# Sharing the tile products of a chunked gated-delta scan between its two directions

## What is computed

```python
def gated_delta_chunked(q, k, v, g, beta, s0):
    # chunks of C tokens; gc = cumsum(g) in a chunk
    decay = exp(where(incl, gc[:, None] - gc[None, :], -inf))
    kb = kc * bc[..., None]
    a_low = where(strict, einsum('cd,sd->cs', kb, kc) * decay, 0)      # key products
    tmat = a_low + eye(C)
    w = solve(tmat, kb * exp(gc)[..., None]); u = solve(tmat, vc * bc[..., None])
    qk = einsum('cd,sd->cs', qc, kc) * decay                           # query-key products
    kd = kc * exp(g_last - gc)[..., None]
    def step(s, ...):
        v_new = u_i - w_i @ s
        o = qg_i @ s + qk_i @ v_new
        s = s * exp(gl_i) + kd_i.T @ v_new
o_forward  = gated_delta_chunked(q, k, v, g[0], beta[0], s)
o_backward = reversed(gated_delta_chunked(reversed q, k, v, g[1], beta[1], s))
```

## Time and profile before

| | |
|---|---|
| runs | 1705.11, 1707.46 and 1711.45 us; median 1707.46 |
| profiled execution | 1704.45 us, span of its instructions 1702.3 us |
| mean granted TensorE clock | 0.983 of full speed |
| busy in the span | TensorE 1618.2 us, VectorE 734.4, ScalarE 466.6, GpSimd 569.8 |
| HBM traffic | 307.31 MB read, 14.71 MB written |
| scan of layer 0 | from about 357 us of the span to about 520 |
| scan of layer 1 | from about 1250 us to 1364 |

### The profile page before, as it was taken

How to read it: one execution, slowest core, us unless ns; L and a number is a source line. 1 busy time by engine, 2 the same in 40 slices (tenths; PEclk the granted TensorE clock), 3 DMA queues, 4 the chain that set the end, 5 groups by cost and what they waited for, 6 DMA issues and landing times. The chain is left out here.

```text
span 1702.3 us, 36038 instructions
## 1 busy us (share of the span) xinstructions
PE 1618.2 (95%) x14725; PEld 1108.7 (65%) x14725; DVE 734.4 (43%) x1515; ACT 466.6 (27%) x1042; POOL 569.8 (33%) x698
## 2 busy tenths in 40 slices
PE   6999999889999999999999999999979999999998
PEld 4577875557887865555556447786668986555544
DVE  4257543345545451121111546744456675224233
ACT  4212433253333131111111231253353322111111
POOL 2656304226566213111110155611538881000000
PEclk9999999999999989999999999999989999999999
DMA  9330100069884249999999302010220035899995
GB/s 337 91 115 26 50 15 28 13 191 289 253 269 176 75 176 338 372 359 360 357 342 344 110 25 75 25 50 17 63 85 24 15 124 209 336 413 407 411 413 227
DMA packets 160358, 323.73 MB, mean 190 GB/s; under 512 B 30153, under 2 KB 118127, under 8 KB 144879
## 3 DMA queue, kind: packets, MB, share of 16 engines
q1 hardware_dynamic: 127584, 287.20, 45.8%
q0 software_dynamic: 7008, 21.74, 4.6%
q10 hardware_dynamic: 25646, 13.12, 2.8%
HBM read 307.31 MB, written 14.71 MB: 189 GB/s over the span
## 5 line engine op out<-in xcount | busy, mean ns | idle before, releaser
L1531 PE MATMUL psum<-ring,arena 128*64 128x256 f32 x1536 | 172.8, 381 | 6.8 <-DVE arena L3131 3.4
L1531 PEld LDWEIGHTS psum<-ring,arena 128*64 128x64 f32 x1536 | 108.6, 137 | 68.3 <-issue 13.4
L3642 POOL DMA_INDIRECT big<-h_rows_lat,idx x16 | 15.7, 981 | 346.1 <-PE psum L1664 174.0
L802 PE MATMUL psum<-hT,ring 128*128 128x256 f32 (+2 forms) x496 | 130.2, 421 | 0.0
L3152 DVE TENSOR_TENSOR arena<-arena,psum 128x384 f32<-128x384 f32 (+1 forms) x32 | 15.6, 487 | 257.6 <-PE psum L1540 158.5
L802 PEld LDWEIGHTS psum<-hT,ring 128*128 128x128 f32 (+1 forms) x496 | 92.7, 188 | 36.9 <-issue 26.6
L3190 DVE SCALAR_TENSOR_TENSOR xT<-psum,modraw,xT 128x512 f32<-128x512 f32 (+1 forms) x136 | 79.7, 621 | 48.6 <-PE psum L1618 33.8
L975 PE MATMUL psum<-hT,ring 128*128 128x256 f32 (+1 forms) x192 | 80.0, 525 | 0.0
L2444 ACT COPY arena<-psum 128x512 f32<-128x512 f32 (+2 forms) x49 | 23.7, 483 | 202.5 <-PE psum L1553 143.4
L1614 PE MATMUL psum<-arena 128*128 128x512 f32 x144 | 65.8, 602 | 4.4 <-DVE arena L3177 2.7
L2754 DVE TENSOR_REDUCE small<-psum 128x1 f32<-128x768 f32 (+1 forms) x40 | 33.9, 849 | 82.3 <-PE psum L996 82.2
(11 more groups left out here) (476 smaller groups left out, 3771.7 us busy)
## 6 DMA issues: line engine op xcount, KB each, us to landing
ring<-in_moe_w_gate SPq DMA_DIRECT2D x64, 1024.0 KB, 9.6
ring<-in_ada_w SPq DMA_DIRECT2D x48, 1024.0 KB, 7.1
ring<-in_moe_w_up SPq DMA_DIRECT2D x32, 1024.0 KB, 10.3
hT<-in_moe_w_down SPq DMA_DIRECT2D x24, 1024.0 KB, 12.7
ring<-in_w_in SPq DMA_DIRECT2D x20, 1024.0 KB, 5.5
big<-in_moe_w_up SPq DMA_DIRECT2D x16, 1024.0 KB, 10.9
sz<-in_moe_w_down SPq DMA_DIRECT2D x16, 1024.0 KB, 12.5
big<-in_moe_w_down SPq DMA_DIRECT2D x16, 1024.0 KB
```

The source lines that it names most:

```text
L802: m = pe.matmul(b[0:c1 - c0, 0:n], lhsT=w[:, k, c0:c1], rhs=hT[:, k, t0:t0 + n], start=k == 0, stop=k == KD - 1)
L1531: m = pe.matmul(b[e * CAP_L:(e + 1) * CAP_L, 0:2 * P], lhsT=xs[:, k, e, 0:CAP_L], rhs=w[e][:, 2 * (k - ks[0]) + q, :], start=k == 0, stop= ...
```

## The change

Three kinds of products are made once for two chunks that use the same tiles. `SHARED` lists them with the first of the two chunks: in layer 0 kr and qk of chunk 0 (used again in chunk 1) and kk of chunk 3 (used again in chunk 4); in layer 1 kk of chunk 3 alone. In the first chunk TensorE makes the product as before; ScalarE copies it from PSUM into a part of mixT that isn't written yet (`kept`), at the beginning of the slot in which TensorE makes it, and the bank is free with that copy. VectorE reads the copy in SBUF, in both chunks. In the second chunk TensorE makes nothing. Waits that asked for a bank to be read ask the semaphore "comb" instead, which VectorE increments after each such piece, and the counts of its earlier users are shifted. Two new waits order the reuse of mixT: ScalarE waits for the reads of qk before it puts kk of chunk 3 there, and VectorE's outputs of chunks 2 and 3 wait for its own reads of kr and kk.

```diff
+SHARED = ((("kr", 0), ("qk", 0), ("kk", 3)), (("kk", 3),))
...
+        def shared_steps(l):
+            order = [x for j in range(NT) for slot in range(len(BETWEEN)) for x in between(j, slot)]
+            return [(what, i, d) for what, i, d in order for w, j in SHARED[l] if what == w and i in (j, j + 1)]
+
+        def kept(l, what, j, d):
+            i = tile_of(d, j)
+            row, col = 2, {"kr": (2, 5), "qk": (3, 4)}.get(what, (0, 1))[i] if i < CT else i
+            if i >= CT and what != "kk":
+                row, col = GH * (what == "qk"), i - CT - 1
+            return mixT[:, row:row + GH, col * P:(col + 1) * P]
+
+        def product_kept(l, what, j):
+            return (what, j) in SHARED[l]
+
+        def product_shared(l, what, j):
+            return (what, j - 1) in SHARED[l]
+
+        def factor_made(eng, l, what, j, d):
+            if product_kept(l, what, j) or product_shared(l, what, j):
+                base = sum(1 + IN_PAIRS + len(shared_steps(x)) for x in range(l)) + 1 + IN_PAIRS
+                eng.wait_ge(sems[l]["comb"], base + shared_steps(l).index((what, j, d)) + 1)
+            else:
+                evacuated(eng, (what, l, j, d))
```

In TensorE's pieces:

```diff
+                    if product_shared(l, what, j):
+                        return
...
-                        evacuated(pe, ("qk", l, j, d))
+                        factor_made(pe, l, "qk", j, d)
...
-                        evacuated(pe, ("kr", l, j, d))
+                        factor_made(pe, l, "kr", j, d)
```

At the beginning of each slot of ScalarE:

```diff
+                    for what, i, d in between(j, slot):
+                        if product_kept(l, what, i):
+                            if i == 3 and l == 0:
+                                for e in range(2):
+                                    factor_made(act, l, "qk", 1, e)
+                            b = product_ready(act, (what, l, i, d)).rearrange("p (h c) -> p h c", h=GH)
+                            read_out(act.copy(kept(l, what, i, d), b), (what, l, i, d))
```

On VectorE (its L2804 also reads the product head by head now, 4 x 128 instead of 512):

```diff
+                def heads_product(what, j, d):
+                    if product_shared(l, what, j):
+                        return kept(l, what, j, d)
+                    if product_kept(l, what, j):
+                        evacuated(dve, (what, l, j, d))
+                        return kept(l, what, j, d)
+                    return product_ready(dve, (what, l, j, d)).rearrange("p (h c) -> p h c", h=GH)
+
+                def factor_done(ins, key):
+                    what, _, j, d = key
+                    if product_shared(l, what, j) or product_kept(l, what, j):
+                        ins.then_inc(s["comb"], 1)
+                    else:
+                        read_out(ins, key)
...
-                        b = product_ready(dve, key).rearrange("p (h c) -> p h c", h=GH)
+                        b = heads_product(what, j, d)
...
                         if j == 2:
+                            for e in range(2):
+                                factor_made(dve, l, "kr", 1, e)
+                        if j == 3:
+                            for e in range(2):
+                                factor_made(dve, l, "kk", 4, e)
```

On GpSimd, in `decays` and in `masks`:

```diff
-                            evacuated(pool, ("kk", l, j - 1, d))
+                            factor_made(pool, l, "kk", j - 1, d)
...
-                        evacuated(pool, ("kk", l, j, d))
+                        factor_made(pool, l, "kk", j, d)
```

More of the change, by code:

```diff
@@ L311, in tokens_made @@
         def tokens_made(eng, l):
-            eng.wait_ge(sems[l]["comb"], l * (1 + IN_PAIRS) + 1)
+            eng.wait_ge(sems[l]["comb"], sum(1 + IN_PAIRS + len(shared_steps(x)) for x in range(l)) + 1)
         def taps_added(eng, l, q):
-            eng.wait_ge(sems[l]["comb"], l * (1 + IN_PAIRS) + 2 + q)
+            eng.wait_ge(sems[l]["comb"], sum(1 + IN_PAIRS + len(shared_steps(x)) for x in range(l)) + 2 + q)
         def middle_taps(l):
@@ L2206, in next_decays @@
                         act.wait_ge(s["eb"], 2 * (j - 2) + d + 1)
-                        evacuated(act, ("kr", l, j - 2, d))
+                        factor_made(act, l, "kr", j - 2, d)
                     if j >= 3:
@@ L2798, in gdn_piece @@
                         dve.tensor_tensor(gAO[j % 2][c, 0:2, :], b[r, 0:2, c], decay[r, 0:2, c], ALU.mult)
-                        read_out(dve.tensor_tensor(gAO[j % 2][r, 2:4, :], b[r, 2:4, c], decay[r, 2:4, c], ALU.mult), key)
+                        factor_done(dve.tensor_tensor(gAO[j % 2][r, 2:4, :], b[r, 2:4, c], decay[r, 2:4, c], ALU.mult), key)
                     elif what == "qk" and use_o:
-                        b = product_ready(dve, key)
+                        b = heads_product(what, j, d)
                         dve.wait_ge(s["dm"], 2 * (j - j_out) + d + 1)
-                        x = gE[j % 2][d].rearrange("p h c -> p (h c)")
-                        read_out(dve.scalar_tensor_tensor(out=x, in0=b, scalar=-1.0, in1=x, op0=ALU.mult, op1=ALU.mult),
-                                 key)
+                        x = gE[j % 2][d]
+                        factor_done(dve.scalar_tensor_tensor(out=x, in0=b, scalar=-1.0, in1=x, op0=ALU.mult, op1=ALU.mult),
+                                    key)
                     elif what == "kr":
-                        b = product_ready(dve, key).rearrange("p (h c) -> p h c", h=GH)
+                        b = heads_product(what, j, d)
                         dve.wait_ge(s["dex"], 2 * j + d + 1)
-                        read_out(dve.scalar_tensor_tensor(
+                        factor_done(dve.scalar_tensor_tensor(
                             out=gKD[d], in0=b, scalar=-1.0,
@@ L2822, in gdn_piece @@
                         o = mixT[:, 2:2 + GH, i * P:(i + 1) * P]
+                        if j == 2:
+                            for e in range(2):
[3 more added lines that the diff above has]
+                                factor_made(dve, l, "kk", 4, e)
                         first = [tile_of(1 - d, x) for x in range(NT)].index(i) > j
```

## The result

The changed kernel takes **1710.64 us** (median of 21 runs, 1704.55 to 1714.51), the kernel before in runs beside it 1707.46 us (21 runs, 1704.24 to 1711.45). The ratio is **1.0018, 95% interval 1.0011 to 1.0026**: 3.2 us slower by the medians, 1.9 to 4.4 by the interval. That is inside the half per cent that the prediction called no change, and inside its range; it is 2.6 us above the number. A few executions in the later tables took 2700 us or more: they stand in the medians, which they move by 0.3 us at most, and not in the ratios.

The account below looks back on a forecast made before the run. TensorE time was taken to bound layer 0's scan, a chain of waits between GpSimd, VectorE and TensorE layer 1's. Terms -2.7 + 0.2 + 3.2 = +0.7 us on 1707.46 gave 1708 us, 8 in 10 within 1701.5 to 1713.

Parts of the forecast that it names:

- Removed work: Layer 0's chunks 1 and 3: dropping 4.9 us of TensorE products gains 2.7 us, the rest turning into waits.
- TensorE being 2.1 us earlier changes none of that: 0.: Layer 1, chunk 4's key products: VectorE waits for GpSimd anyway, so removing 2.1 us of TensorE gains 0.
- The wait for a bank: Layer 1: TensorE's 1.50 us wait for a bank VectorE reads should go, without use.
- Copies: ScalarE's eight added copies, 582 ns each, 4.7 us in all: only 0.2 us charged, in layer 0's chunk 0.
- Collisions: VectorE reads with two SBUF operands stretch beside GpSimd in both layers' scans: 3.2 us lost, 2.1 of it in layer 1.
- A: Rival: GpSimd and VectorE don't disturb each other in the scans; 1705 us, chance 0.19.
- B: Rival: all removed TensorE time counts in both layers, -7.0 us; 1700.5 us, chance 0.07.
- C: Rival: every moved VectorE instruction meeting a GpSimd one waits for all of it; 1717.5 us, half 1712.5; chance 0.15.

Follow-up runs that it names:

- layer 0 alone: The change made in layer 0 only, layer 1 as in the kernel before: 1704.97 us, ratio 0.9998 to the kernel before.
- Read in PSUM: The whole change, but VectorE reads the first chunk's product in PSUM and only the second chunk reads ScalarE's copy: 1708.61 us, ratio 1.0005 to before.
- layer 1 alone: The change made in layer 1 only, layer 0 as in the kernel before: 1708.97 us, ratio 1.0012 to the kernel before.
- whole, pauses filled: The whole change plus one idle 512-column matmul in each of four TensorE pauses of layer 1: 1707.88 us, ratio 1.0006 to before.

## Why the prediction was right, and where it was not

- **Removed work.** Counts as forecast. Layer 0 was to give 2.7 us less 1.3 for its copies and collisions, so 1.4. Its scan gave 3.9 to 4.1 in two traces (1.3 where a half-clock stretch fell into it, and none where rows came late). By chunks, in those two traces against the mean of the two of before: chunk 0 to 1 forecast -1.2, measured -2.1, and TensorE waited 1.0 and 1.1 us before the value product, as forecast (1 us or more). Two waits before L1165, 1.08 and 0.89 us in one profile of before and 0.81 and 0.61 in the other, are 0.6 and 0.3 in the second profile of after. Chunk 2 to 3 forecast -0.6, measured -0.85; chunks 1 to 2 and 3 to 4, where +0.4 and nothing was forecast, gave 0.35 and 0.6. The two profiles of before differ in such a step by up to 0.8 us (26.92 and 27.68 for chunk 3 to 4), so the sum is firmer than its parts. The term was too small; that TensorE is more of a bound there than the prediction took it for fits, but no run shows it.
- **Layer 1: "TensorE being 2.1 us earlier changes none of that: 0."** This is the step that failed. True for the elementwise chain, but the missing 2.1 us and a longer pause had an effect of their own: 3.4 us of half clock in two places. I had read the clock column as 1.00 in every window of the scan from chunk 1 on and never asked what would keep it there.
- **The wait for a bank.** The 1.50 us before L1125 did go, without use, as forecast. It joined the next wait: 2.23 us before the value product.
- **Copies.** 599 ns each, forecast 582. In layer 1 they cost nothing that shows: with all copies kept, only moving an operand brought the 0.28 us back. In chunk 2 of layer 0 VectorE waits 0.93 and 1.07 us for a copy (layer 0 alone), where it waited 0.22 us or not at all for TensorE, and that step still isn't longer than before (26.92 us against 27.34).
- **Collisions.** The forecast said 1.5 and 0.6 us in layer 1's chunks 2 and 3; measured 1.4 and 0.8. In layer 0 it charged 1.1 us (0.6, 0.3, 0.1 and 0.1), and no run shows what of that is lost. The stretching is there: in chunk 3 the six instructions take 2.51 us instead of 2.05, and in chunk 1 the two query-key reads take 2.04, where chunk 2's, in PSUM, take 1.28 (layer 0 alone). But only the terms of 0.1 were put to the test, and brought nothing. The masks came 7.8 us after the first key instruction, forecast 7.9.
- **Sum.** Forecast: layer 0 -1.4, layer 1 +2.1, so +0.7. The scans in the traces: layer 0 -1.3 and layer 1 +5.5 in the first pair, -4.1 and +5.6 in the second, so +4.2 and +1.5 us, against 3.2 (1.9 to 4.4) by the runs. That the number was so near is luck: two mis-sized terms, of 2.5 and 3.4 us, stood against each other. What carried the forecast of no change is that both were small.
- **Rivals.** A had no collisions: out. B, all of the removed work counts: nearly true of layer 0's scan (3.85 of 4.9), out in layer 1. C, each collision a whole wait: true of the single instruction that meets L3485, but only one of six meets it, and the copies of 0.4 us cost a share. Its 1712.5 lies above the interval of the measured ratio.

Alone, the layers' ratios come out milder than their scans: layer 0 -0.3 us (-2.2 to +1.4) against -3.85, layer 1 +2.0 (0.3 to 3.8) against +4.0. So the gain of layer 0's scan is not shown to reach the end of the program. In the profile of layer 0 alone the code between the scans takes 1.3 to 2.2 us longer than in those of before, and the code behind layer 1's scan 3.1 to 4.3 us longer (the table at the end), though no edit touches either.

## What to carry to other kernels

Work taken from an engine with slack is not free of effect when that engine's clock depends on what it does: look for the pauses that the removal opens or joins, and at the clock in the windows behind them. Before an operand is moved from PSUM to SBUF, lay the reader's timeline over GpSimd's: in these traces a VectorE instruction with both operands in SBUF that starts behind a GpSimd one of 1.04 us ends just after it (1.11 us instead of 0.28), and the same instruction with one operand in PSUM doesn't wait. A gain in one stage is kept only if what follows lets it through: look at the stages behind it too. A copy made for a later use need not serve the first.

## What the runs showed that was not expected

**The clock of an engine that is over nine tenths busy hangs on single pauses.** Before, TensorE waits 1.50 us for the bank and 1.25 us for the masks in chunk 2 and for neither in chunk 3, and keeps 2.4 GHz. After, it waits 2.23 us before the value product and 1.48 for the masks in chunk 2, 1.28 and 1.49 in chunk 3, and each time the clock is halved some 5 us after the value product. Read in PSUM, chunk 2 has 1.41 and 1.26 us and keeps its clock; chunk 3 has 1.40 and 1.44 and doesn't. So the waits alone, added up, don't decide it: their places and the products missing between them differ too, and these runs don't separate that. One idle matmul in each pause was enough.

**Untouched code can change its pace with the kernel.** Near the end, in the experts' part of layer 1, which no edit touches, the same step recurs six times (from 1464.61 to 1645.30 us before). Its 180.69 us are 181.49 after and 181.48 in the second profile, 182.25 with layer 0 alone, 180.52 with layer 1 alone. Part of the difference sits in a wait for VectorE, 0.39 us a step before and 0.49 after:

```profile
L1614 PE MATMUL psum<-arena x30: 592/592/668, 1503.8 to 1539.6; 128*128 128x512 f32 x30
its engine sat idle before it (us, times) until:
  DVE arena L3177: 0.8, 2
```
```profile
L1646 PE MATMUL psum<-arena x31: 592/592/668, 1513.6 to 1549.9; 128*128 128x512 f32 x31
its engine sat idle before it (us, times) until:
  DVE arena L3239: 1.0, 2
```

Layer 0 alone has the same 0.49 us and a still longer step, so the wait is not all of it. And the whole change loses nothing by it: the step across the end of these six, from one first start of L1614 to the next (1624.30 to 1655.28 us before), takes 30.98 and 31.71 us before and 30.25 after. From the first of eight such starts to the last it is 211.81 and 212.40 us before, 211.44 and 211.43 after. The cause of the pace stays open.

**The rest of the difference between the traces** lies mostly in parts that no edit touches (us; layer 1's chunk 0 to 1 is between value products, "between" from the last value product of layer 0 to the first of layer 1, "behind" from the last one of layer 1 to the first L1614):

| | between | chunk 0 to 1 | behind | first to last L1614 |
|---|---|---|---|---|
| before, two profiles | 740.90, 741.77 | 19.20, 19.25 | 115.56, 114.35 | 211.81, 212.40 |
| whole change, two profiles | 743.15, 742.70 | 20.90, 20.93 | 116.85, 117.31 | 211.44, 211.43 |
| layer 0 alone | 743.11 | 17.61 | 118.61 | 212.15 |
| layer 1 alone | 741.53 | 19.01 | 119.26 | 211.58 |
| whole, pauses filled, two profiles | 742.94, 740.14 | 20.94, 17.62 | 116.61, 116.94 | 211.43, 211.78 |

Chunk 0 to 1 of layer 1 takes 17.6, 19.2 or 20.9 us as it holds no half clock, one stretch of 3.4 us or some 9.5 us of it. Both pairs show 1.7 us more there for the whole change; but the kernel with filled pauses, whose code there is the same, has 20.9 in one profile and 17.6 in the other. Half-clock stretches come and go in other untouched places too: one at 574.1 us stands in the second profile of before and not in the first, one at 1033.1 us in the second of the whole change and not in the first. The part ahead of layer 0's first value product takes 383.28 and 381.99 us before, 383.45 and 384.21 after. Whether the change makes them more frequent there, two profiles of each can't say.
